# Attention on one Trainium2 core: mask sums, exponents and turned probabilities over 23 or 31 key columns instead of 24 or 32

## The chip, the cores and the metric

The kernel runs on one core of one Trainium2 chip. The time is device microseconds of one execution of the whole program. Before the change the median of three runs is 2007.32 us (2007.18 to 2007.69).

## The reference

The program computes a two-layer encoder on 1024 tokens of width 1024, in fp32. The tokens lie on a grid of 16 rows of 64 columns. In each layer eight heads of 64 features attend to a neighbourhood; other heads mix by a gated spatial matrix and by a Fourier transform; a projection and a SwiGLU feed-forward part follow. The part that matters here:

```python
kh, kw = 8, 16                     # each query sees 8 rows of 16 columns, clamped inside the grid
sc = einsum('bhjqd,bkjnhd->bhjqkn', q_row, k_band) * scale
logits = sc + bias                 # relative-position table; -1e9 outside the window
p = softmax(logits, axis=-1)
o = einsum('bhjqkn,bkjnhd->bjqhd', p, v_band)
```

## The kernel before, in words

Nearly all products are fp32 split into a high and a low part, three products for one. The attention of a layer lies between the last input product and the output projection. It is cut into eight tiles (`TILES`, line 56) of 128 queries: 8 grid rows by 16 grid columns. A tile is (j, rr): j is one of four column groups, rr the upper or the lower half of the rows. A tile's keys are 11 or 12 grid rows (`KR`) of `KC[j]` columns that start at column `BAND[j]`: 24, 32, 32 and 24 columns. So a head of a tile has 264, 288, 352 or 384 keys. They are worked in three chunks of four grid rows (`chunk`), 96 or 128 keys each, and the last one of an 11-row tile is shorter.

Work goes by pairs of heads, 32 pairs per layer (i in the code, four per tile). For each pair:

- TensorE makes the scores of both heads (`scores`, L2398, six products into two banks).
- VectorE adds the relative-position table and takes the negative maximum in one instruction per head (`logits`, L1772), reading the scores from PSUM and the table from SBUF and writing SBUF.
- ScalarE takes the exponent in place and its sum (`probs`, L1189).
- TensorE turns the probabilities chunk by chunk, 64 queries at a time (`turn_halves`, L2547; for the very first pair `turn_probs`, L2450).
- VectorE and ScalarE copy the turned halves to SBUF (L1809, L1214; first pair L1806, L1211).
- TensorE multiplies with the values (`values`, L2470): two heads, three chunks, six products, which the profile lists as twelve (two passes each).

After a tile VectorE, ScalarE and GpSimd norm its heads and TensorE turns them twice (L2485, L2492).

TensorE's order is written out by hand and it works in that order: `scores(i)`, `values(i - 2)`, sometimes a turn of other heads (`turn_batch`), `turn_halves(i - 1)`; from the fifth pair of pairs on (m in the code) two pairs at a time. An instruction that waits holds up all that is behind it on its engine.

The values come through DRAM: they are stored as `v_scratch` and loaded again with keys on partitions, by `load_rows(j)` (L678 to L682), one call for each column group. It has two buffers, `VB[j % 2]`. A call is four DMAs, one for each grid row modulo 4; each fills `KC[j]` partitions, from partition `r * KC[j]`, with four pieces of 512 floats (2048 bytes) per partition:

```python
sp.dma_start(VB[j % 2][r * KC[j]:(r + 1) * KC[j], :, :],
             vscr.rearrange("(n r w) d -> r w n d", r=CHUNK_ROWS, w=GW)[
                 r, BAND[j]:BAND[j] + KC[j]]).then_inc(vb_landed[j % 2], 16)
```

SyncE's queue issues in this order, and waits in it too: `load_rows(0)` when the values are stored; the tables of the third tile (its first half after four heads' mask sums of tile 0, its second half after eight); `load_rows(1)` once four batches are turned; the tables of the fourth tile; the first output weights; four 1 MB loads of the residual (`X`); `load_rows(2)` when the first two tiles' value products are done (`pv_done`), since it overwrites the first buffer; `load_rows(3)` when the next two tiles' are; the last tables. `values` waits for `vb_landed` before the first, third, fifth and seventh tile, that is for i = 0, 8, 16 and 24.

The relative-position tables (`bias`, laid out on the host by `lay_out`) have `KC[j]` columns per key row as well, are loaded by `load_bias` (L684 to L694) over 128 partitions, and are read by L1772.

Of the kernel before, what the change touches and what calls it, by code (L numbers as in the profile page):

```python
# [27 lines left out]
P = 128  # L28
# [3 lines left out]
DH = 64  # L32
# [12 lines left out]
KH, KW = 8, 16  # L45
QR, QC = 8, 16
KR = [11, 12]
KC = [24, 32, 32, 24]
CHUNK_ROWS = 4
NCHUNK = 3  # L50
NKEY = KR[1] * KC[1]
NJ = GW // QC
COMBO = [0, 1, 1, 2]
BAND = [min(max(QC * j - KW // 2, 0), GW - KC[j]) for j in range(NJ)]
NEG = -1e9
TILES = [(0, 1), (0, 0), (1, 0), (1, 1), (2, 1), (2, 0), (3, 0), (3, 1)]
BIAS_BUF = [0, 1, 0, 1, 1, 0, 1, 0]
# [129 lines left out]
def build(nc, x, win, wout, wom, wg, wu, wd, bias, wsp, bsp, lng, lnb, gmix, ghead, gffn, gfin,  # L187
          tw, bd, ident, out):
    ctx = ExitStack()
    with ctx:  # L190
        def at(name, kb, shape, dt=F32):
            return nc.alloc_sbuf_tensor_at(name, shape, dt, offset=BASE + int(kb * KB))
# [15 lines left out]
        MB, MC = UV[:, 0], XC[:, :, :]  # L208
        BIAS = [at(f"bias{n}", AT[f"BIAS{n}"], [P, 2, HA // 2 * NKEY]) for n in range(2)]
        SQB = [at(f"mix_sq{n}", AT[f"SQB{n}"], [P, 8, WB]) for n in range(2)]  # L210
# [14 lines left out]
        TW = at("twiddle", AT["TW"], [P, 5, 2, 256])  # L225
        L = at("logits", AT["L"], [P, 4, NKEY])
        OC = at("att_heads", AT["OT"], [P, NP, P])
# [26 lines left out]
        small = [200 * KB]  # L254
# [9 lines left out]
        shared = small[0]  # L264
# [8 lines left out]
        MV = keep("mean_var", [P, 8, 2])  # L273
        LR = keep("ln_rstd", [P, 8])
        PT = nc.alloc_sbuf_tensor_at("probs_t", [P, 4 * NCHUNK, P], F32, offset=BASE + shared)
        small[0] = shared + 4 * NKEY * 4
        for n, name in enumerate(("cu", "u4u", "t4")):
            HID[name] = nc.alloc_sbuf_tensor_at(f"hid_{name}", [P, HALF], F32, offset=BASE + shared + n * HALF * 4)
        GM = keep("g_mix", [P, KT_D])
# [14 lines left out]
        B = [ctx.enter_context(nc.psum_tensor(f"bank{i}", [P, HALF], F32)) for i in range(8)]  # L294

        def sem(name):
            return ctx.enter_context(nc.semaphore(name))
# [32 lines left out]
        s_full, l_made, p_made, pt_full, pt_dve, pt_act, pv_done = (  # L330
            sem(x) for x in ("s_full", "l_made", "p_made", "pt_full", "pt_dve", "pt_act", "pv_done"))
# [33 lines left out]
        def grid(ap):  # L365
            return ap.rearrange("p (r c) -> p r c", c=GW)
# [46 lines left out]
        def wait_tapped(e, l, n, j):  # L413

            if n == Z_GELU:
                e.wait_ge(z_ev, l * 8 + j + 1)
            elif n in ACT_TAPS:
                e.wait_ge(tap_act, l * 4 * len(ACT_TAPS) + 4 * ACT_TAPS.index(n) + j + 1)
            else:
                e.wait_ge(tap_dve, l * 4 * len(DVE_TAPS) + 4 * DVE_TAPS.index(n) + j + 1)  # L420
# [64 lines left out]
        def q_view(t, b):  # L485

            return t[:, b // 2, :].rearrange("p (j h r c) -> p h r j c", j=NJ, h=2, c=QC)[:, b % 2]

        def q_bank(b, ap):
            return ap.rearrange("p (r j c) -> p r j c", j=NJ, c=QC)  # L490

        BATCHES = [4, 5, 6, 7, 0, 1, 2, 3]
        BATCH_BANK = [4, 5, 7, 4, 5, 7, 4, 7]
        SINGLE = 8
# [14 lines left out]
        def keys(tile):  # L509
            j, rr = TILES[tile]  # L510
            return KR[rr] * KC[j]

        def chunk(tile, n):

            w = CHUNK_ROWS * KC[TILES[tile][0]]
            return slice(n * w, min((n + 1) * w, keys(tile)))

        def chunk_keys(tile, n):
            c = chunk(tile, n)
            return c.stop - c.start  # L520

        def score_bank(i, e):

            return B[e + 4 * (i >= SINGLE and i % 2)][:, 0:keys(i // 4)]

        def head_probs(t, n=None):

            first = t % 4 * NCHUNK
            return PT[:, first:first + NCHUNK, :] if n is None else PT[:, first + n, :]

        def half_probs(i, e):

            return PT[:, 2 * (i % 2) * NCHUNK:2 * (i % 2 + 1) * NCHUNK, e * DH:(e + 1) * DH]

        def turns_done(t):

            return t + 1 if t < 2 * WHOLE else t - t % 2 + 2
# [12 lines left out]
        def _(sp):  # L550
# [90 lines left out]
            for l in range(DEPTH):  # L641
# [36 lines left out]
                def load_rows(j):  # L678
                    for r in range(CHUNK_ROWS):
# [4 lines that stand above are left out]
# [225 lines left out]
        def _(act):  # L909
# [151 lines left out]
            for l in range(DEPTH):  # L1061
# [143 lines left out]
                def turned_odd(t):  # L1205
                    act.wait_ge(pt_full, l * 64 + t + 1)
                    if t >= 4:
                        act.wait_ge(pv_done, l * 64 + t - 3)
                    w = chunk_keys(t // 8, 0)
                    if t < 2 * WHOLE:  # L1210
                        nc.scalar.activation(head_probs(t)[0:w], B[3][0:w, 0:NKEY].rearrange("p (n q) -> p n q", q=P),  # L1211
                                             ACT.Copy).then_inc(pt_act, 1)
                    else:
                        nc.scalar.activation(half_probs(t // 2, 1)[0:w],  # L1214
                                             B[3][0:w, 0:NKEY].rearrange("p (g q) -> p g q", q=DH),
                                             ACT.Copy).then_inc(pt_act, 1)

                def batch_hi(i):
# [18 lines left out]
                for i in range(SINGLE):  # L1237
# [8 lines left out]
                    if 1 <= i < 5:  # L1246
                        c = i - 1
# [98 lines left out]
                for r in range(DN_STEPS):  # L1346
# [8 lines left out]
                    i = r - 58  # L1355
# [22 lines left out]
        def _(dve):  # L1378
# [136 lines left out]
            for l in range(DEPTH):  # L1515
# [126 lines left out]
                c = 0.5 ** 0.5  # L1642
# [119 lines left out]
                def logits(t):  # L1762

                    tile, h = divmod(t, 8)
                    dve.wait_ge(s_full, l * 64 + t + 1)
                    if t >= 4:
                        dve.wait_ge(pt_full, l * 64 + turns_done(t - 4))
                    if h % 4 == 0:
                        dve.wait_ge(bias_landed[BIAS_BUF[tile]][h // 4], l * 48 + 16 * BIAS_NTH[tile])
                    dve.sem_inc(dve_passed, 1)  # L1770

                    nc.vector.tensor_tensor_reduce(  # L1772
                        L[:, t % 4, 0:keys(tile)], score_bank(t // 2, t % 2),
                        BIAS[BIAS_BUF[tile]][:, h // 4, h % 4 * keys(tile):(h % 4 + 1) * keys(tile)], -1.0, 3e38,
                        ALU.add, ALU.min, NM[:, t % 4:t % 4 + 1]).then_inc(l_made, 1)

                logits(0)
                logits(1)
                tap(13, 2)
                head_norm(1, MB, SQB[0][:, :, :])  # L1780
# [19 lines left out]
                def turned_even(t):  # L1800
                    dve.wait_ge(pt_full, l * 64 + t + 1)
                    if t >= 4:
                        dve.wait_ge(pv_done, l * 64 + t - 2)
                    w = chunk_keys(t // 8, 0)
                    if t < 2 * WHOLE:
                        nc.vector.tensor_copy(head_probs(t)[0:w], B[2][0:w, 0:NKEY].rearrange("p (n q) -> p n q", q=P))\  # L1806
                            .then_inc(pt_dve, 1)
                    else:
                        nc.vector.tensor_copy(half_probs(t // 2, 0)[0:w],  # L1809
                                              B[2][0:w, 0:NKEY].rearrange("p (g q) -> p g q", q=DH)).then_inc(pt_dve, 1)  # L1810

                def batch_lo(i):
                    b = BATCHES[i]
# [367 lines left out]
                for r in range(DN_STEPS):  # L2181
# [3 lines left out]
                    i = r - 59  # L2185
# [37 lines left out]
        def _(pe):  # L2223
# [29 lines left out]
            for l in range(DEPTH):  # L2253
# [33 lines left out]
                for i, (k, h) in enumerate(X_ORDER):  # L2287
# [5 lines left out]
                    w = slice(k % 4 * WB, (k % 4 + 1) * WB)  # L2293
# [86 lines left out]
                def scores(i):  # L2380
                    tile, c = divmod(i, 4)
                    j, rr = TILES[tile]
                    if i > SINGLE + 1:
                        pe.wait_ge(l_made, l * 64 + 2 * i - 2)
                    elif i > SINGLE:
                        pe.wait_ge(bt_lo, l * 8 + 7)
                    elif i:
                        pe.wait_ge(l_made, l * 64 + 2 * i)
                    else:
                        pe.wait_ge(qk_lo, l * 16 + 12)  # L2390
                        wait_tapped(pe, l, NPROD - 1, 1)
                    if 4 <= i < 8:
                        pe.wait_ge(qk_lo, l * 16 + 8 + i + 1)
                    q0 = (2 * j + rr) * P
                    for n, (qs, ks) in enumerate(((QH, KH_), (QH, KL), (QL, KH_))):
                        for e in range(2):
                            hp = slice(DH * e, DH * e + DH)
                            mm = nc.tensor.matmul(  # L2398
                                score_bank(i, e).rearrange("p (r c) -> p r c", c=KC[j]), qs[hp, c, q0:q0 + P],
                                grid(ks[hp, c, :])[:, 4 * rr:4 * rr + KR[rr], BAND[j]:BAND[j] + KC[j]],  # L2400
                                start=n == 0, stop=n == 2)
                            if n == 2:
                                mm.then_inc(s_full, 1)
# [438 lines left out]
```

## Time and profile before

| | |
|---|---|
| median of the runs | 2007.32 us |
| the profiled execution | 2007.3 us |
| its span, first to last instruction | 2005.5 us |
| TensorE busy | 1981.8 us, 99% |
| VectorE busy | 1530.2 us, 76% |
| ScalarE busy | 895.3 us, 45% |
| GpSimd busy | 221.0 us, 11% |
| mean granted TensorE clock | 0.999 |

The profile is one execution on the chip. PE is TensorE's matmuls, PEld its weight loads, DVE VectorE, ACT ScalarE, POOL GpSimd, SPq SyncE's DMA queue. Times are in microseconds from the start of the span unless marked ns. An engine's busy time is a sum over stages with different limits, so the attention stages are read by themselves: the first is at about 198 to 276 us, the second at about 1189 to 1267 us. The share of DMA is the mean busy share of the core's 16 DMA engines; packets that overlap make it a little over 100% at times.

### The profile page before, as it was taken

The numbers are of one execution on the slowest core, as the hardware profiler recorded it, in microseconds if no ns is written. First come the engines' busy times: TensorE is split into PE (matmuls) and PEld (weight loads), VectorE is DVE, ScalarE is ACT, GpSimd is POOL, SyncE is SP. The second block draws the span as 40 slices with busy tenths as digits, with TensorE's granted clock in tenths as the row PEclk, the third lists the DMA queues.
The fourth block names the chain that finished last, engine by engine and source line by source line (L and its number), as shares of the span: only waits on it lengthen the run. The fifth ranks groups of instructions, "written<-read, shape, count | busy, mean of one in ns | idle before, by whom it ended". The sixth has DMA issues, their size and how long they took to land.

```text
span 2005.5 us, 28816 instructions
## 1 busy us (share of the span) xinstructions
PE 1981.8 (99%) x10528; PEld 1647.2 (82%) x10528; DVE 1530.2 (76%) x2511; ACT 895.3 (45%) x1611; POOL 221.0 (11%) x156
## 2 busy tenths in 40 slices
PE   8999999999999999999999999999999999999998
PEld 7887788888888888888898877888888888888887
DVE  8847874799777777787777488567997777778877
ACT  7453873443333333444544549535333333344443
POOL 1221453100000000000013123630000000000000
PEclk9999999999999999999999999999999999999999
DMA  7965743124432338533477668331343233293333
GB/s 247 214 168 154 228 156 119 43 99 170 132 110 90 106 109 288 174 98 96 120 220 193 156 159 245 138 105 58 129 157 118 90 106 110 100 342 99 95 100 122
DMA packets 130988, 288.91 MB, mean 144 GB/s; under 512 B 12960, under 2 KB 17952, under 8 KB 130592
## 3 DMA queue, kind: packets, MB, share of 16 engines
q1 hardware_dynamic: 107584, 241.97, 37.0%
q0 software_dynamic: 10880, 20.97, 6.3%
q10 hardware_dynamic: 12384, 24.12, 3.4%
q8 instruction: 85, 1.39, 0.3%
q14 instruction: 55, 0.45, 0.1%
HBM read 227.77 MB, written 59.24 MB: 143 GB/s over the span
## 4 chain that ended last, share of the span: by engine, by line
PE 89%; DVE 6%; issue 2%; ACT 2%; DMA 0%; DVEq 0%; SPq 0%; ACTq 0%
PE bank L2249 27%; PE bank L2251 27%; PE bank L2250 27%; PE bank L2470 1%; PE bank L2398 1%; PE bank L2547 1%; DVE s_lo L1484 1%; DVE t_lo L1913 0%; PE bank L2492 0%; PE bank L2361 0%; PE bank L2485 0%; ACT logits L1189 0%; PE bank L2377 0%; DVE logits L1772 0%; DVE att_sq L1829 0%
## 5 line engine op out<-in xcount | busy, mean ns | idle before, releaser
L2249 PE MATMUL bank<-t_hi,s_hi 128*128 128x512 f32 (+1 forms) x1336 | 516.9, 387 | 0.8 <-DVE hid_cu L2026 0.5
L2250 PE MATMUL bank<-t_lo,s_hi 128*128 128x512 f32 (+1 forms) x1336 | 516.3, 386 | 0.0
L2251 PE MATMUL bank<-t_hi,s_lo 128*128 128x512 f32 (+1 forms) x1336 | 516.3, 386 | 0.0
L2249 PEld LDWEIGHTS bank<-t_hi,s_hi 128*128 128x128 f32 x1336 | 250.9, 188 | 52.4 <-DVE hid_cu L2026 1.3
L2251 PEld LDWEIGHTS bank<-t_hi,s_lo 128*128 128x128 f32 x1336 | 250.9, 188 | 50.9
L2250 PEld LDWEIGHTS bank<-t_lo,s_hi 128*128 128x128 f32 x1336 | 251.0, 188 | 50.7
L2249 PE MATMUL bank<-b_hi,s_hi 128*128 128x512 f32 x528 | 206.0, 390 | 0.1
L2251 PE MATMUL bank<-b_hi,s_lo 128*128 128x512 f32 x528 | 205.5, 389 | 0.0
L2250 PE MATMUL bank<-b_lo,s_hi 128*128 128x512 f32 x528 | 205.4, 389 | 0.0
L992 ACT ACTIVATE s_hi<-w_u 128x512 fp32r<-128x512 f32 x142 | 89.6, 631 | 233.1 <-PE bank L2251 175.6
L992 ACT ACTIVATE s_hi<-w_down 128x512 fp32r<-128x512 f32 x154 | 97.3, 632 | 201.9 <-PE bank L2251 199.9
L1484 DVE TENSOR_TENSOR s_lo<-w_down,s_hi 128x512 fp32r<-128x512 f32 x154 | 107.7, 700 | 76.9 <-ACT s_hi L992 76.9
L992 ACT ACTIVATE s_hi<-w_g 128x512 fp32r<-128x512 f32 x142 | 89.4, 630 | 163.2 <-PE bank L2251 104.1
L827 POOL TENSOR_TENSOR w_lo<-w_raw,w_hi 128x1024 fp32r<-128x1024 f32 x34 | 85.7, 2532 | 691.8 <-ACT w_hi L932 580.1
L932 ACT ACTIVATE w_hi<-w_raw 128x1024 fp32r<-128x1024 f32 x91 | 92.8, 1053 | 68.3 <-DMA w_raw<-in_win 48.9
L2249 PEld LDWEIGHTS bank<-b_hi,s_hi 128*128 128x128 f32 x528 | 99.1, 188 | 21.3 <-issue 0.9
L2251 PEld LDWEIGHTS bank<-b_hi,s_lo 128*128 128x128 f32 x528 | 99.1, 188 | 20.7
L2250 PEld LDWEIGHTS bank<-b_lo,s_hi 128*128 128x128 f32 x528 | 99.2, 188 | 20.3
L1494 DVE TENSOR_TENSOR t_lo<-t_raw,t_hi 128x512 fp32r<-128x512 f32 x154 | 105.7, 687 | 6.3 <-ACT t_hi L998 6.1
L1484 DVE TENSOR_TENSOR s_lo<-w_g,s_hi 128x512 fp32r<-128x512 f32 x142 | 97.5, 686 | 10.6 <-ACT s_hi L992 10.6
L2249 PE MATMUL bank<-h_hi,w_hi 128*128 128x512 f32 x256 | 101.1, 395 | 0.0
L2251 PE MATMUL bank<-h_hi,w_lo 128*128 128x512 f32 x256 | 99.8, 390 | 0.0
(296 smaller groups left out, 3704.8 us busy)
## 6 DMA issues: line engine op xcount, KB each, us to landing
w_raw<-in_win SPq DMA_DIRECT2D x51, 512.0 KB, 5.8
w_g<-in_wg SPq DMA_DIRECT2D x44, 512.0 KB, 3.6
w_u<-in_wu SPq DMA_DIRECT2D x44, 512.0 KB, 4.5
t_raw<-hidden_t SPq DMA_DIRECT2D x88, 256.0 KB, 2.6
w_raw<-in_win POOLq DMA_DIRECT2D x40, 512.0 KB, 7.1
t_raw<-hidden_b SPq DMA_DIRECT2D x66, 256.0 KB, 2.6
hidden_b<-hid_g SPq DMA_DIRECT2D x60, 256.0 KB, 2.0
hidden_t<-hid_x SPq DMA_DIRECT2D x44, 256.0 KB, 2.0
```

The lines of the kernel that those rows point to most:

```text
L827: nc.gpsimd.tensor_tensor(WL[s][:, :], WR[s][:, :], WH[s][:, :], ALU.subtract).then_inc(w_ready, 1)
L932: nc.scalar.activation(WH[s][:, :], WR[s][:, :], ACT.Copy).then_inc(w_hi, 1)
L992: nc.scalar.activation(SH[q % W_RING][:, :], weight_block(q), ACT.Copy).then_inc(s_hi, 1)
L1484: nc.vector.tensor_tensor(SL[q % W_RING][:, :], weight_block(q), SH[q % W_RING][:, :], ALU.subtract)\
L1494: nc.vector.tensor_tensor(TL[t][:, :], TR[t][:, :], TH[t][:, :], ALU.subtract).then_inc(t_lo, 1)
L2249: nc.tensor.matmul(bank, lh, rh, start=start, stop=False, skip_group_check=reopened)
L2250: nc.tensor.matmul(bank, lh, rl, start=False, stop=False, skip_group_check=reopened)
L2251: return nc.tensor.matmul(bank, ll, rh, start=False, stop=stop, skip_group_check=reopened)
L2398: mm = nc.tensor.matmul(score_bank(i, e).rearrange("p (r c) -> p r c", c=KC[j]), qs[hp, c, q0:q0 + P], grid(ks[hp, c, :])[:, 4 * rr:4 * rr ...
L2470: mm = nc.tensor.matmul(B[VALUE_BANK][e * DH:(e + 1) * DH, c * P:(c + 1) * P], VB[j % 2][0:w, rr + n, h * DH:(h + 1) * DH], head_probs(h, ...
L2547: mm = nc.tensor.transpose(B[2 + e][0:chunk_keys(t // 8, n), (NCHUNK * s + n) * DH:(NCHUNK * s + n + 1) * DH], L[rows, t % 4, chunk(t // 8 ...
```

## The change

Column groups 0, 1 and 2 are cut to 23, 31 and 31 key columns (`KC`); their 24th or 32nd column is in no query's window. Group 3 keeps 24. The scores are still computed for 24, 32, 32 and 24 columns (`KS`) into the same places in PSUM. The mask sum reads from PSUM 23 or 31 of each 24 or 32 columns and writes rows of 23 or 31 without gaps. All that is sized by `KC`, and so needs no edit of its own, follows: the exponents, the chunks (92 or 124 keys), the turned probabilities, the value products, the tables in DRAM and their loads, and the partitions that `load_rows` fills. `NTURN` takes the place of `NKEY` where 384 turned elements are meant; the copies move what they moved, on 92 or 124 partitions.

```diff
-KC = [24, 32, 32, 24]
+KC = [23, 31, 31, 24]
+KS = [24, 32, 32, 24]
 CHUNK_ROWS = 4
 NCHUNK = 3
 NKEY = KR[1] * KC[1]
+NTURN = NCHUNK * P
@@
-        small[0] = shared + 4 * NKEY * 4
+        small[0] = shared + 4 * NTURN * 4
@@
         def score_bank(i, e):
-            return B[e + 4 * (i >= SINGLE and i % 2)][:, 0:keys(i // 4)]
+            j, rr = TILES[i // 4]
+            bank = B[e + 4 * (i >= SINGLE and i % 2)]
+            return bank[:, 0:KR[rr] * KS[j]].rearrange("p (r c) -> p r c", c=KS[j])
@@
-                        nc.scalar.activation(head_probs(t)[0:w], B[3][0:w, 0:NKEY].rearrange("p (n q) -> p n q", q=P),
+                        nc.scalar.activation(head_probs(t)[0:w], B[3][0:w, 0:NTURN].rearrange("p (n q) -> p n q", q=P),
@@
+                    def by_row(ap):
+                        return ap.rearrange("p (r c) -> p r c", c=KC[TILES[tile][0]])
+
                     nc.vector.tensor_tensor_reduce(
-                        L[:, t % 4, 0:keys(tile)], score_bank(t // 2, t % 2),
-                        BIAS[BIAS_BUF[tile]][:, h // 4, h % 4 * keys(tile):(h % 4 + 1) * keys(tile)], -1.0, 3e38,
+                        by_row(L[:, t % 4, 0:keys(tile)]), score_bank(t // 2, t % 2)[:, :, 0:KC[TILES[tile][0]]],
+                        by_row(BIAS[BIAS_BUF[tile]][:, h // 4, h % 4 * keys(tile):(h % 4 + 1) * keys(tile)]), -1.0, 3e38,
                         ALU.add, ALU.min, NM[:, t % 4:t % 4 + 1]).then_inc(l_made, 1)
@@
                             mm = nc.tensor.matmul(
-                                score_bank(i, e).rearrange("p (r c) -> p r c", c=KC[j]), qs[hp, c, q0:q0 + P],
-                                grid(ks[hp, c, :])[:, 4 * rr:4 * rr + KR[rr], BAND[j]:BAND[j] + KC[j]],
+                                score_bank(i, e), qs[hp, c, q0:q0 + P],
+                                grid(ks[hp, c, :])[:, 4 * rr:4 * rr + KR[rr], BAND[j]:BAND[j] + KS[j]],
                                 start=n == 0, stop=n == 2)
```

The other copies of turned probabilities get `NTURN` for `NKEY` in the same way. No instruction is added or removed, and no wait.

## Rows read from the trace of the kernel before

**Rows 1.** The page: busy time by engine, and the chain that ended last.
```profile
...
PE 1981.8 (99%) x10528; PEld 1647.2 (82%) x10528; DVE 1530.2 (76%) x2511; ACT 895.3 (45%) x1611; POOL 221.0 (11%) x156
...
PE 89%; DVE 6%; issue 2%; ACT 2%; DMA 0%; DVEq 0%; SPq 0%; ACTq 0%
...
```

**Rows 2.** Stretch of the first attention: busy us (instructions) per engine, clock, DMA, GB/s.
```profile
...
198.00:276.00 78.00, 74.38 (x1027) 59.86 (x1026) 67.43 (x193) 67.67 (x187) 27.32 (x25) 1.00 0.69 201
```

**Rows 3.** Groups by shape, same stretch: busy us, mean ns | idle before, releaser.
```profile
...
L1772 DVE CUSTOM_DVE_ANT_0 logits<-bank,bias 128x384 f32<-128x384 f32 x16 | 8.4, 551 | 0.4 <-PE bank L2398 0.4
L1772 DVE CUSTOM_DVE_ANT_0 logits<-bank,bias 128x264 f32<-128x264 f32 x16 | 6.3, 425 | 0.0
L1189 ACT ACTIVATE logits<-logits,minus_max 128x384 f32<-128x384 f32 x16 | 9.7, 608 | 0.7 <-DVE minus_max L1772 0.7
L1189 ACT ACTIVATE logits<-logits,minus_max 128x264 f32<-128x264 f32 x16 | 8.2, 511 | 1.1 <-DVE minus_max L1772 1.1
L2547 PE MATMUL bank<-ident,logits 64*128 64x64 f32 x160 | 8.9, 231 | 0.3 <-issue 0.2
L2547 PE MATMUL bank<-ident,logits 64*96 64x64 f32 x168 | 10.4, 222 | 0.0
L2470 PE MATMUL bank<-probs_t,v_band 128*64 128x128 f32 x160 | 11.6, 279 | 0.0
L2470 PE MATMUL bank<-probs_t,v_band 96*64 96x128 f32 x168 | 13.5, 279 | 1.6 <-ACT probs_t L1214 1.2 <-DVE probs_t L1809 0.2
...
```

**Rows 4.** Timeline of SyncE's queue, first layer: start, us from first to last issue.
```profile
...
198.35 1.57 SPq L680 DMA_DIRECT2D v_band<-v_scratch  x4
205.95 6.79 SPq L693 DMA_DIRECT2D bias<-in_bias  x2
212.78 2.10 SPq L680 DMA_DIRECT2D v_band<-v_scratch  x4
218.14 6.07 SPq L693 DMA_DIRECT2D bias<-in_bias  x2
...
224.72 2.28 SPq L710 DMA_DIRECT2D x_res<-in_x  x4
227.72 3.90 SPq L680 DMA_DIRECT2D v_band<-v_scratch  x4
```

**Rows 5.** Timeline of TensorE: first value products of tiles 0, 2 and 4.
```profile
...
208.00 0.88 PE L2470 MATMUL bank<-probs_t,v_band 96*64 96x128 f32 x12
...
229.84 1.07 PE L2470 MATMUL bank<-probs_t,v_band 128*64 128x128 f32 x14
...
247.19 1.08 PE L2470 MATMUL bank<-probs_t,v_band 128*64 128x128 f32 x14
```

**Rows 6.** DMA, 200.5 to 203.5 us: `load_rows(0)` moves, alone; queue: packets, MB, share.
```profile
...
DMA packets 275, 0.50 MB, mean 167 GB/s; under 512 B 30, under 2 KB 30, under 8 KB 275
...
q1 hardware_dynamic: 275, 0.50, 79.4%
...
```

**Rows 7.** DMA, 216.5 to 219.5 us: `load_rows(1)` moves.
```profile
...
DMA packets 355, 0.67 MB, mean 223 GB/s; under 512 B 38, under 2 KB 38, under 8 KB 353
...
q1 hardware_dynamic: 353, 0.65, 104.7%
...
```

**Rows 8.** DMA, 1192 to 1195.5 us: `load_rows(0)` of the second layer.
```profile
...
q1 hardware_dynamic: 342, 0.62, 74.9%
...
```

**Rows 9.** DMA, 770 to 780 us: feed-forward weights, pieces of 2048 bytes.
```profile
...
DMA packets 1985, 3.86 MB, mean 386 GB/s; under 512 B 99, under 2 KB 99, under 8 KB 1985
...
```

**Rows 10.** DMA, 229 to 236 us: the residual's loads.
```profile
...
q1 hardware_dynamic: 739, 2.88, 100.9%
...
```

**Rows 11.** Two stretches after the program's first matmul, columns as in rows 2.
```profile
...
7.00:10.00 3.00, 3.00 (x15) 3.00 (x16) 2.36 (x4) 3.00 (x6) 0.00 (x0) 1.00 1.03 367
11.00:14.00 3.00, 3.00 (x27) 3.00 (x27) 3.00 (x5) 3.00 (x5) 0.00 (x0) 1.00 1.05 387
...
```

More of the change, by code:

```diff
@@ L1214, in turned_odd @@
                         nc.scalar.activation(half_probs(t // 2, 1)[0:w],
-                                             B[3][0:w, 0:NKEY].rearrange("p (g q) -> p g q", q=DH),
+                                             B[3][0:w, 0:NTURN].rearrange("p (g q) -> p g q", q=DH),
                                              ACT.Copy).then_inc(pt_act, 1)
@@ L1805, in turned_even @@
                     if t < 2 * WHOLE:
-                        nc.vector.tensor_copy(head_probs(t)[0:w], B[2][0:w, 0:NKEY].rearrange("p (n q) -> p n q", q=P))\
+                        nc.vector.tensor_copy(head_probs(t)[0:w], B[2][0:w, 0:NTURN].rearrange("p (n q) -> p n q", q=P))\
                             .then_inc(pt_dve, 1)
@@ L1809, in turned_even @@
                         nc.vector.tensor_copy(half_probs(t // 2, 0)[0:w],
-                                              B[2][0:w, 0:NKEY].rearrange("p (g q) -> p g q", q=DH)).then_inc(pt_dve, 1)
+                                              B[2][0:w, 0:NTURN].rearrange("p (g q) -> p g q", q=DH)).then_inc(pt_dve, 1)
                 def batch_lo(i):
```

## The prediction

> **What bounds the kernel now.** I read the page first: TensorE is busy for 99% of the span and holds 89% of the chain that ended last [rows 1]. Then the stretch of the attention by itself, since the change is only there. In 78 us TensorE is busy 74.4, VectorE 67.4 and ScalarE 67.7 [rows 2]: three engines that hand heads to each other, none with much slack. The reader should see that a saving on one of them is worth at most itself. Next the groups by shape give the price of an element [rows 3]. Last, because the mask, the chunks and the value rows are sized by one constant, I read the loads that this constant also sizes: SyncE's queue in order of time [rows 4], the moments at which TensorE needs the value bands [rows 5], and the DMA engines while the bands move [rows 6 to 8].
>
> **The edits that were meant.** Mask sum: 384 keys take 551 ns and 264 take 425, so 1.05 ns a key [rows 3]. A 12-row tile loses 12 keys, an 11-row tile 11; 24 heads of each per layer give 24 x 12.6 + 24 x 11.6 = 0.58 us, 1.16 us in two layers. Exponent: (608 - 511) / 120 = 0.81 ns a key, 0.9 us in two layers [rows 3]. Turns: 128 columns take 231 ns, 96 take 222, so four columns are worth about 1.1 ns; 12 per pair of heads, 24 pairs, two layers: 0.6 us [rows 3]. Value products: 128 and 96 keys both take 279 ns, so nothing [rows 3]. The copies of turned probabilities move 384 elements as before, on fewer partitions: nothing, by the same reading. If all of this lay in series on the path it would be 2.7 us. It does not, the three engines overlap; I would take 1 us. The mask sum now reads PSUM in rows with a gap. No row of before shows that form at this line. Its bounds are nothing and one more element per row, 12 x 1.05 = 12.6 ns a head, which would just cancel its saving; I take nothing. The scores are as they were. The table loads keep 128 partitions and shrink by 3 or 4%: nothing.
>
> **The edit that comes along.** `load_rows` (L680) fills `KC[j]` partitions per DMA. That was 24 or 32 and becomes 23 or 31. How many DMA engines such a transfer uses can be read off. While the 24-partition loads move alone, the share is 79.4% in one layer and 74.9% in the other [rows 6, 8]; while the 32-partition loads move it is 104.7% [rows 7]. Their ratio is 0.72 to 0.76, and 12 of 16 engines is 0.75. The small packets agree. Packets under 512 B I take for the writes that report an engine's part as done, since no tile is moved in such pieces there. In [rows 6] there are 30 of them beside 245 others, one per 8.2 pieces. A 24-partition load has 24 x 4 = 96 pieces: on 12 engines 8 each, on 16 engines it would be 6. In [rows 7] it is 315 to 38, one per 8.3; 32 x 4 / 16 = 8. So each engine takes an equal share of whole partitions, and 12 and 16 are the largest counts up to 16 that divide 24 and 32. By that reading 23 and 31, which are primes, go to a single engine. The other reading that fits is two partitions per engine with an odd last share; nothing in these rows shows an uneven share. The Trainium skill (DMA: Bandwidth & Descriptors, section "Why a DMA increments its semaphore by 16 and not by 1") says that the hardware takes the largest count up to 16 that divides the slowest dimension of both sides, with 127 partitions on one engine as its example; the trace agrees for 24 and 32, and no row here shows a prime count. By that rule the sum below stands; by the other reading it would be that of rival (a).
>
> The price of a piece on one engine. The nearest clean row is the stretch of 2048-byte pieces at 770 us: 3.86 MB in 10 us on 16 engines, 0.0241 MB per engine and us, so 85 ns a piece [rows 9]. While the bands move it is worse: 0.794 x 3 us x 16 / 245 = 156 ns [rows 6]. There twelve engines write into 24 partitions at once; one engine by itself meets no such company, so I take 85 ns and keep 156 as the other end.
>
> The sum for the first layer, on the times of [rows 4, 5]:
> - `load_rows(0)`: 4 x 23 x 4 = 368 pieces x 85 ns = 31.3 us, from 198.35, with 1 us put on for start and landing (a guess): 230.7. The first value product stood at 208.00. TensorE waits, and scores, turns and all that VectorE and ScalarE live on are queued behind: a stall of 22.7 us.
> - `load_rows(1)` was issued at 212.78, 4.8 us after that product, because SyncE first waits for mask sums and turned batches that are behind it. So it comes at 235.5. Ahead of it on the same engine are 8 table rows of 5.5 KB, 44 KB, 2 us at the rate of [rows 10]. Then 4 x 31 x 4 = 496 pieces, 42.2 us, and 1 us: 280.6. Tile 2 needed it at 229.84 + 22.7 = 252.5: a stall of 28.1 us.
> - `load_rows(2)` was issued at 227.72 and comes at 250.4, while the engine is busy until 279.6. Ahead of it are that engine's parts of the tables of tile 3 (16 rows, 4 us), of the output weights (1.3) and of the residual: 4 MB / 16 at 2.88 MB per 7 us and 16 engines [rows 10] is 10.2 us. Then 42.2 and 1: 338 us. Tile 4 would follow tile 2 by 247.19 - 229.84 = 17.35 us, at 298.0: a stall of 40 us.
> - `load_rows(3)` keeps 24 partitions and its 12 engines, and follows at once. It is needed 17 us later: nothing.
>
> That is 91 us a layer, and 182 for both, since the second layer issues the same queue. The small savings of the first paragraph disappear under it: these stretches are bound by one DMA engine.
>
> A stall has a second cost. After its first 6.8 us without work TensorE ran 15 matmuls in 3 us, later 27 in 3 us of the same kind [rows 11], so it restarts at about half pace and loses some 1.7 us. The column of the granted clock says 1.00 in both, so the cause is not settled by it. The restart of tile 2 is covered by the load it waits for next; those of tiles 0 and 4 move the path: 3.4 us a layer, 7 us in all.
>
> Sum: the profiled execution has 2005.5 us of span and 1.8 us around it, 2007.3, which is also the median. 2007.3 + 182 + 7 = 2196.
>
> **The rivals.** (a) The loads spread as before, with an uneven last share. Then a band still moves in about 5 us, 0.75 MB at 0.50 MB in 3 us [rows 6], and what is left are the meant edits: 2007.3 - 1 = 2006.3, at best 2004.6. This is the case that is not slower; it decides by one thing, the share of DMA while `load_rows` moves. For it: 24 and 32 partitions had exactly two per engine. Against it: no uneven share in the trace. (b) One engine, but pieces at the 156 ns of [rows 6]. The bands take 57.4, 77.4 and 77.4 us: first band 256.8, a stall of 48.8; second 342, a stall of 63; third 435, a stall of 76; 188 a layer, 2390 in all with the restarts. For it: the only row in which these very bytes move. Against it: that row has many engines on few partitions. (c) The spread stays and the gapped rows cost VectorE more than I bound: for 0.2% it would have to be 4.0 us / 96 heads = 42 ns a head, beyond the bound. (d) The change is faster by over 0.2%: that needs 4.0 us, and all meant savings in series are 2.7.
>
> **How the numbers follow.** A change of 0.2%, 4 us, is about what can be told from none. Forecast with one engine near 85 ns: 0.68, 2196 us. (b), or a rate between: 0.14, up to 2390. (a): 0.11. (c) and other slower cases, such as few engines in place of one: 0.05. (d): 0.02. Slower is 0.68 + 0.14 + 0.05 = 0.87, same 0.11, faster 0.02. For the range, the lower bound of the forecast is the case in which the tables, weights and residual do not hold the third band up (15.5 us a layer) and restarts cost nothing: 2196 - 31 - 7 = 2158; a little less for a margin, 2145. The upper end is that of (b), 2390. It leaves out (a), (c), (d) and a sliver, under 2 in 10.
>
> **What the profile after would show.** While `load_rows(0)` moves the DMA share is near 1/16 = 6% for some 31 us, not 79% for 5; 3 stalls per layer before L2470, of about 23, 28 and 40 us, with `v_band` as what ended them; L1772 about 12 ns and L1189 about 10 ns shorter for 372 and 341 keys, for 276 and 253 too; L2470 unchanged at 279 ns; the fourth band as before. The prediction falls if the share during the bands stays above 70%, and its size falls if a piece takes other than 85 ns.

## The result and the profile after

The changed kernel takes 2206.95 us (median of four runs, 2206.15 to 2207.68) where the kernel before took 2007.39 us (median of four). The ratio is 1.099, with a 95% interval of 1.098 to 1.101. The profiled execution has a span of 2205.9 us. That is 199.6 us slower by the medians, 200.4 us by the spans.

The page after, with busy time, granted clock and the chain that ended last:

```profile
PE 1996.3 (90%) x10528; PEld 1661.4 (75%) x10528; DVE 1528.8 (69%) x2511; ACT 895.6 (41%) x1611; POOL 221.2 (10%) x156
...
PEclk9999668999999999999999986699999999999999
...
PE 78%; SPq 8%; DVE 6%; DMA 6%; issue 2%; ACT 1%; DVEq 0%; ACTq 0%
PE bank L2256 24%; PE bank L2258 24%; PE bank L2257 24%; SPq L684 6%; DMA v_band<-v_scratch 5%; SPq L697 1%; PE bank L2477 1%; SPq L714 1%; PE bank L2554 1%; DVE s_lo L1488 1%; PE bank L2405 1%; DMA v_scratch<-v_tok 0%; DVE t_lo L1920 0%; PE bank L2368 0%; PE bank L2499 0%
```

TensorE's share fell from 99% [rows 1] to 90%, and the clock row, all nines before, has two dips. SyncE's queue (SPq), its line L684 and the band of values are new in the chain. L684 is `load_rows`.

The list of waits names one new wait on TensorE. The columns are total us, times, longest:

```profile
PE bank L2477 <- DMA v_band<-v_scratch: 188.7, 6, 38.5
```

Six waits, three per layer, 188.7 of the 200.4 us. TensorE's timeline gives each by its place. These are the first value products of tiles 0, 2 and 4, which stood at 208.00, 229.84 and 247.19 before [rows 5]; the bracket is the idle time before them and its releaser:

```profile
231.24 1.55 PE L2477 MATMUL bank<-probs_t,v_band 92*64 92x128 f32 x12 [23.22 <-DMA v_band<-v_scratch]
...
286.52 1.76 PE L2477 MATMUL bank<-probs_t,v_band 124*64 124x128 f32 x14 [31.79 <-DMA v_band<-v_scratch]
...
344.35 2.40 PE L2477 MATMUL bank<-probs_t,v_band 124*64 124x128 f32 x20 [38.34 <-DMA v_band<-v_scratch]
```

SyncE's queue, which issued these loads at 198.35, 212.78 and 227.72 before [rows 4] (start, us from first to last issue):

```profile
198.08 15.80 SPq L684 DMA_DIRECT2D v_band<-v_scratch  x4
213.98 23.43 SPq L697 DMA_DIRECT2D bias<-in_bias  x2
237.45 24.96 SPq L684 DMA_DIRECT2D v_band<-v_scratch  x4
262.46 10.71 SPq L697 DMA_DIRECT2D bias<-in_bias  x2
...
273.86 8.74 SPq L714 DMA_DIRECT2D x_res<-in_x  x4
282.64 51.75 SPq L684 DMA_DIRECT2D v_band<-v_scratch  x8
```

And the DMA queue in the same three microseconds as rows 6:

```profile
DMA packets 35, 0.08 MB, mean 26 GB/s; under 512 B 0, under 2 KB 0, under 8 KB 34
...
q1 hardware_dynamic: 34, 0.07, 6.0%
```

Where 12 engines were busy (79.4%), about one is: 6.0% of 16 is 0.96 of an engine. There are 34 packets in 3 us, one every 88 ns.

The groups by shape answer to rows 3. The stretch holds stalls and half-clock work here, so TensorE's means are not those of an undisturbed stage:

```profile
L2477 PE MATMUL bank<-probs_t,v_band 124*64 124x128 f32 x160 | 13.7, 315 | 70.1 <-DMA v_band<-v_scratch 70.1
...
L1193 ACT ACTIVATE logits<-logits,minus_max 128x372 f32<-128x372 f32 x16 | 9.5, 599 | 1.3 <-DVE minus_max L1779 1.3
...
L2554 PE MATMUL bank<-ident,logits 64*124 64x64 f32 x160 | 9.4, 239 | 0.2
...
L1779 DVE CUSTOM_DVE_ANT_0 logits<-bank,bias 128x372 f32<-128x372 f32 x16 | 8.2, 539 | 0.7 <-PE bank L2405 0.7
```

The mask sum went from 551 to 539 ns and the exponent from 608 to 599. The meant edits did what they say, in a stage that now waits for something else.

### The profile page after: what moved, and what is told of

It is laid out like the page before. It is cut to its first block, busy times and chain, and to the rows that moved or that the text cites. A ratio compares the mean times of both kernels' runs of the same rounds, so it can differ in the third digit from the quotient of the medians.

```text
span 2205.9 us, 28816 instructions
## 1 busy us (share of the span) xinstructions
PE 1996.3 (90%) x10528; PEld 1661.4 (75%) x10528; DVE 1528.8 (69%) x2511; ACT 895.6 (41%) x1611; POOL 221.2 (10%) x156
## 4 chain that ended last, share of the span: by engine, by line
PE 78%; SPq 8%; DVE 6%; DMA 6%; issue 2%; ACT 1%; DVEq 0%; ACTq 0%
PE bank L2256 24%; PE bank L2258 24%; PE bank L2257 24%; SPq L684 6%; DMA v_band<-v_scratch 5%; SPq L697 1%; PE bank L2477 1%; SPq L714 1%; PE bank L2554 1%; DVE s_lo L1488 1%; PE bank L2405 1%; DMA v_scratch<-v_tok 0%; DVE t_lo L1920 0%; PE bank L2368 0%; PE bank L2499 0%
## 5 line engine op out<-in xcount | busy, mean ns | idle before, releaser
L2477 PE MATMUL bank<-probs_t,v_band 124*64 124x128 f32 (+5 forms) x768 | 58.9, 304 | 190.4 <-DMA v_band<-v_scratch 188.7
L2477 PEld LDWEIGHTS bank<-probs_t,v_band 124*64 124x64 f32 (+5 forms) x768 | 47.8, 152 | 197.9 <-issue 193.5
L1816 DVE COPY probs_t<-bank 124x384 f32<-124x384 f32 (+2 forms) x62 | 34.3, 553 | 211.0 <-PE bank L2554 210.4
L1218 ACT ACTIVATE probs_t<-bank 124x384 f32<-124x384 f32 (+2 forms) x62 | 29.7, 479 | 204.5 <-PE bank L2554 204.3
```

What stands on the lines that cost most here:

```text
L1218: nc.scalar.activation(half_probs(t // 2, 1)[0:w], B[3][0:w, 0:NTURN].rearrange("p (g q) -> p g q", q=DH), ACT.Copy).then_inc(pt_act, 1)
L1816: nc.vector.tensor_copy(half_probs(t // 2, 0)[0:w], B[2][0:w, 0:NTURN].rearrange("p (g q) -> p g q", q=DH)).then_inc(pt_dve, 1)
L2477: mm = nc.tensor.matmul(B[VALUE_BANK][e * DH:(e + 1) * DH, c * P:(c + 1) * P], VB[j % 2][0:w, rr + n, h * DH:(h + 1) * DH], head_probs(h, ...
```

## The experiments

**Part by part: only the first group, only the middle groups.** Both kernels differ from the changed one in one line.

```diff
-KC = [23, 31, 31, 24]
+KC = [23, 32, 32, 24]      # e3_only_23
+KC = [24, 31, 31, 24]      # e4_only_31
```

> The changed kernel with KC = 23, 32, 32, 24: only the first band is loaded over a prime number of partitions. Theory: the first stall of each layer stays (23 us) and the other two go; with 3 us for TensorE's slower restart that is 2007 + 2 x 26 = 2059 us. Rival, that the stalls come from something all narrowed tiles share: the time scales with the number of narrowed heads, 2 of 6 tiles, 2007 + 200 / 3 = 2074 us, and stalls stand before tiles 2 and 4 too.

> The changed kernel with KC = 24, 31, 31, 24: the first band loads as before. Theory: no first stall; the second band is issued at 212.8 us and lands near 212.8 + 3 + 42 = 258 us, needed at 230: a stall of 28 us; the third is queued behind it, the residual and the tables and lands near 317, needed at 275: 41 us. 2007 + 2 x (28 + 41 + 3) = 2151 us. Rival of shared cause: 4 of 6 tiles, 2007 + 133 = 2140 us, with stalls inside the tiles and not only before the value products of tiles 2 and 4.

Measured: 2060.1 us and 2156.4 us. The waits for the bands, first of e3_only_23 and then of e4_only_31:

```profile
PE bank L2477 <- DMA v_band<-v_scratch: 46.8, 2, 23.6
```

```profile
PE bank L2477 <- DMA v_band<-v_scratch: 142.8, 4, 39.4
```

Two waits of 23 us with 23 columns, four of 32 to 39 us with 31, and none where the load is over 24 or 32 partitions. The two parts add up: 52.8 + 149.1 = 201.9 us against 199.6 together. The expectations were 2059 and 2151 us. The rivals of a shared cause (2074 and 2140 us) fall, on the time by 14 and 16 us and on the place of the waits.

**The load alone, computation untouched.**

```diff
+PART = {24: 23, 32: 31}
-                        sp.dma_start(VB[j % 2][r * KC[j]:(r + 1) * KC[j], :, :], ...)
+                        for a, b in ((0, PART[KC[j]]), (PART[KC[j]], KC[j])):
+                            sp.dma_start(VB[j % 2][r * KC[j] + a:r * KC[j] + b, :, :], ...)
```

(In TensorE's wait for the band, eight loads are counted instead of four.)

> The kernel before, masks, chunks and sums untouched, with each band load of 32 partitions cut into 31 and 1, and each of 24 into 23 and 1. Theory: 31, 23 and 1 all go to one engine, which then moves 384, 512 and 512 pieces for 368, 496 and 496; 16 pieces more are 1.4 us per band, 8 us in all, and the meant savings of 1 us are absent: 2207 + 9 = 2216 us. Rival, the narrowed computation is part of the cost: clearly below 2207 us.

Measured: 2243.2 us. With masks, chunks and sums as before, the loss is there in full: nothing that was narrowed is needed for it. The waits for bands over the whole run:

```profile
PE bank L2472 <- DMA v_band<-v_scratch: 180.8, 6, 35.5
```

The size I missed, by 27 us. The sum of the expectation left out what the fourth band costs, which the edit cuts too, 24 partitions into 23 and 1, and which the changed kernel does not. What that does in the first layer stands in the stretch from 350 to 390 us, in which there is a wait that is not for a band at all:

```profile
DVE logits L1774 <- DMA bias<-in_bias: 19.3, 1, 19.3
PEld bank L2472 <- DVE probs_t L1811: 18.8, 1, 18.8
```

SyncE's queue shows why. The columns are start and us from first to last issue:

```profile
283.12 79.68 SPq L682 DMA_DIRECT2D v_band<-v_scratch  x16
362.85 2.80 SPq L695 DMA_DIRECT2D bias<-in_bias  x4
```

The 16 issues of the third and fourth band stretch over 80 us (part of it is the wait for value products between the two), and the tables of the last tiles, issued at 362.85, come too late for VectorE's mask sum. Over both layers VectorE waits 39.2 us for these tables, in two waits. A load on one engine costs whoever is behind it in the queue that issues it, and not only who waits for its data.

**The load mended, computation as changed.** Each load is cut in two by the loop of e2_before_31_1, so that by the largest divisor each part goes to 11 to 16 engines:

```diff
+PART = {23: 12, 31: 16, 24: 12}    # e1_split, on the changed kernel: 12+11, 16+15, 12+12
+PART = {24: 12, 32: 16}            # e5_before_16_16, on the kernel before: 12+12, 16+16
```

> The changed kernel with each band load of 31 partitions cut into loads of 16 and 15, of 23 into 12 and 11, of 24 into 12 and 12 (eight loads a band instead of four). Theory, one engine for a prime number of partitions: every load then spreads over 11 to 16 engines, a band moves in about 5 to 8 us, the six stalls before the value products go, and the time falls from 2207 us to that of the kernel before less the meant savings, 2005 to 2008 us. Rival, the mask sums over rows with gaps or the odd chunk sizes hold the path: the time stays above 2050 us, and mask sums of 372 keys or turns are slower than the 539 and 239 ns they took in the changed kernel.

> The kernel before with its band loads cut in two (32 into 16 and 16, 24 into 12 and 12), nothing else. It is the control of e1_split: whatever eight loads in place of four cost is in both. Expected within 0.1% of before (2006 to 2009 us), since each engine moves the same pieces. e1_split against this one is the meant edits alone: theory 1 us faster (2.7 at most), rival nothing or slower.

Measured: 2008.24 us for e1_split (2006.66 to 2011.73, ratio 1.0005, interval 0.9996 to 1.0014) and 2008.63 us for its control (ratio 1.0012, 1.0003 to 1.0021). The first is 0.2 us above the 2005 to 2008 us that I expected. The six stalls are gone, and of 189 us of waits for bands one is left in e1_split:

```profile
PE bank L2479 <- DMA v_band<-v_scratch: 1.0, 1, 1.0
```

Both kernels scatter over 5 and 9 us where the kernel before scatters over 1.2 us, so they don't resolve an edit worth 1 us. The control is 1.3 us slower than before, and its interval leaves 1 out, so there the cut is not free.

**A looser third band.** The same pair with the residual's four loads issued behind the third band's load, and the changed kernel itself with that order alone:

```diff
-                for k in range(0, KT_D, 2): sp.dma_start(X[:, k:k + 2, :], ...)
-                for j in (2, 3):
-                    sp.wait_ge(pv_done, l * 64 + 16 * (j - 1))
-                    load_rows(j)
+                sp.wait_ge(pv_done, l * 64 + 16)
+                load_rows(2)
+                for k in range(0, KT_D, 2): sp.dma_start(X[:, k:k + 2, :], ...)
+                sp.wait_ge(pv_done, l * 64 + 32)
+                load_rows(3)
```

> The changed kernel with cut band loads (as e1_split) and the four loads of the residual issued behind the third band's load instead of ahead of it, so that the third band no longer lands only half a us before its use. Theory: the meant edits then show, at most 2.7 us and about 1: 2005.5 us. Rival: the path through the attention is TensorE's own work, which the edits leave alone, and the time is that of its control e9_before_split_x_behind within 0.3 us.

> The kernel before with the same cut loads (16 and 16, 12 and 12) and the residual's loads behind the third band's: the control of e8_split_x_behind. Theory: what the cut cost in e5_before_16_16 (1.3 us) was the third band landing too late, so this one is back at 2006.5 to 2007.3 us with a narrow spread. Rival: the cost is the eight issues themselves, and it stays at 2008.5.

> The changed kernel, band loads as they are in it, with the four loads of the residual issued behind the third band's load. Theory, the residual's share of engine 0 (10 us) stands ahead of the third band, and slows the tail of the second by some 2 us: both go, 12 us a layer, 2183 us. Rival, only the pieces of the bands themselves count: 2207 us.

Measured: e8_split_x_behind 2007.00 us (2006.53 to 2008.41; ratio 0.9998, 0.9989 to 1.0007), its control 2009.41 us (2006.81 to 2013.07; ratio 1.0010, 1.0002 to 1.0019). The control did not come back to 2007 and still scatters, so the theory that the cut's cost was the third band's lateness falls; its rival, the eight issues, gave 2008.5. I had expected e8_split_x_behind at 2005.5 us, 1.5 us less than it took. What makes the control scatter is open. The pair differs by 2.4 us in favour of the narrowed kernel, but with a control that moves by 6 us I don't take that for the worth of the edits. Neither beats the kernel before by more than the measurement tells.

e7_x_behind took 2189.5 us, 17.4 less than the changed kernel, where I expected 24. First value products of tiles 2 and 4:

```profile
283.43 0.91 PE L2478 MATMUL bank<-probs_t,v_band 124*64 124x128 f32 x6 [26.00 <-DMA v_band<-v_scratch]
...
334.22 2.19 PE L2478 MATMUL bank<-probs_t,v_band 124*64 124x128 f32 x18 [31.14 <-DMA v_band<-v_scratch]
```

The third stall fell from 38.3 to 31.1 us. The second band landed 3.1 us earlier (283.43 for 286.52) and the third 10.1 us earlier (334.22 for 344.35), where 12 was expected. So the residual's share of that one engine was part of the cost, as the sum had it. The rival, that only the bands' pieces count, falls.

The second stall fell by 5.8 us, more than the 3.1 us of its band, and the rest is not the edit. After the first stall TensorE's granted clock stays 0.50 until about 245 us in this profile, and until 237 in that of the changed kernel, though nothing ahead of it differs. So TensorE comes to the second wait 2.7 us later. e2_before_31_1 and e3_only_23, with the same first stall, also show 0.50 until about 245. How long the low clock lasts behind the same stall varies between executions, and here the next wait hides it.

**Which rule gives the number of engines.**

```diff
+                        for a, b in {24: ((0, 24),), 32: ((0, 25), (25, 32))}[KC[j]]:
```

> The kernel before with each band load of 32 partitions cut into 25 and 7; those of 24 stay whole. Three readings of how many engines a load gets. Largest count up to 16 that divides the partitions: 5 and 7 engines; the fullest engine moves 20 + 4 = 24 pieces per grid row, 96 a band, 8 us at 85 ns. The second band still lands in time, the third lands 2 to 6 us late: 2010 to 2020 us. One engine whenever the count is not a multiple of 8: 128 pieces per grid row on engine 0 and stalls like those of the changed kernel in the second and third band, about 2150 us. Uneven shares on all engines: within 2 us of before.

Measured: 2028.1 us (2027.08 to 2029.62; ratio 1.011, 1.009 to 1.012). While the second band moves:

```profile
DMA packets 220, 0.44 MB, mean 147 GB/s; under 512 B 18, under 2 KB 18, under 8 KB 218
...
q1 hardware_dynamic: 218, 0.42, 42.0%
```

42.0% of 16 engines are 6.7: between the one engine of a non-multiple of 8 and the 16 of uneven shares, and near the 7 of the largest divisor, if the 5 engines of one part are among the 7 of the other. The small packets say the same. 128 pieces of a grid row, as 25 and 7 partitions on 5 and 7 engines, would end in 12 of them, one per 10.7; on one engine for each part in 2, one per 64; with two partitions per engine and an odd last share in 13 and 4, one per 7.5. The row has 18 beside 202, one per 11.2. The waits for bands:

```profile
PE bank L2471 <- DMA v_band<-v_scratch: 17.2, 2, 9.2
```

This picks the largest divisor among the three readings. The size is above the 2010 to 2020 us I gave: the third band ended 9.2 and 8.0 us late. I had priced its pieces at 85 ns, and the row above says otherwise: 202 data packets in 0.42 x 3 us x 16 are 100 ns each, before the load meets the residual's and the tables'.

**The meant edits alone.** The bands are loaded as before, in shape and in place:

```diff
-                        sp.dma_start(VB[j % 2][r * KC[j]:(r + 1) * KC[j], :, :], ... r, BAND[j]:BAND[j] + KC[j]
+                        sp.dma_start(VB[j % 2][r * KS[j]:(r + 1) * KS[j], :, :], ... r, BAND[j]:BAND[j] + KS[j]
```

> The changed kernel with band loads of 24 and 32 partitions, four a band and exactly as before, each grid row at its old partition. Left out: the value products then multiply some keys with the wrong value rows, so the attention's output is not the reference's; no instruction, shape or wait differs from the changed kernel but the loads. It is the meant edits alone, without the wide spread that cut loads brought. Theory: about 1 us faster than before, 2006.3 us, at most 2.7 us. Rival, odd starts, rows with gaps or chunks of 92 and 124 cost something: 2007.5 us or more.

Measured: 2007.09 us (2006.76 to 2008.96) against 2007.35 us, ratio 0.9999, interval 0.9991 to 1.0008. By shape in its first attention:

```profile
L2477 PE MATMUL bank<-probs_t,v_band 124*64 124x128 f32 x160 | 11.6, 279 | 0.0
L1193 ACT ACTIVATE logits<-logits,minus_max 128x372 f32<-128x372 f32 x16 | 9.6, 600 | 0.8 <-DVE minus_max L1779 0.7
...
L2554 PE MATMUL bank<-ident,logits 64*124 64x64 f32 x160 | 8.8, 228 | 0.2
L1779 DVE CUSTOM_DVE_ANT_0 logits<-bank,bias 128x372 f32<-128x372 f32 x16 | 8.2, 539 | 0.4 <-PE bank L2405 0.4
```

Against rows 3 the mask sum is 12 ns shorter, the exponent 8, the turn 3, the value product the same. The total lies between the 2006.3 us of the theory and the 2007.5 of the rival, and its interval includes no change at all. The last value products of the second attention start here, first e11_wide_bands, then the kernel before:

```profile
1269.42 1.53 PE L2477 MATMUL bank<-probs_t,v_band 96*64 96x128 f32 x24
```

```profile
1269.82 1.53 PE L2470 MATMUL bank<-probs_t,v_band 96*64 96x128 f32 x24
```

That is 0.40 us earlier, with two layers' narrowed heads behind it. But it is one profiled execution of each, and the runs of the kernel before alone differ by 0.9 us. It hints at less than the 1 us that I took, and doesn't show a gain. This kernel was made for its time only; a right one that loads the wide bands was not built.

**TensorE's clock.** The changed kernel with small matmuls in front of the three waits, and each wait moved behind TensorE's other waits of that place:

```diff
+                        for _ in range({0: 150, 8: 210, 16: 255, 24: 0}[i]):     # e10_busy
+                        for _ in range({0: 100, 8: 132, 16: 172, 24: 0}[i]):     # e12_busy_less
+                            nc.tensor.matmul(B[VALUE_BANK][:, 0:P], IDENT[:, :], IDENT[:, :], start=True, stop=True)
                         pe.wait_ge(vb_landed[j % 2], ...)
```

> The changed kernel with 150, 210 and 255 small fp32 matmuls (identity by identity, into the bank that the value products overwrite next) in TensorE's queue ahead of the waits for the first, second and third band, so that TensorE is not idle while it waits. Theory, part of the 11 us that the stalls do not explain is TensorE at half clock after each: the granted clock stays 1.00 and the time falls by 4 to 10 us, to 2197 to 2203 us. Rival, the extra is something else (queues filling up again): no change, or longer by what the added matmuls overrun.

> As e10_busy, with 100, 132 and 172 of the small matmuls ahead of the waits for the first, second and third band: at 0.225 us each, as e10_busy showed, 22.5, 29.7 and 38.7 us, just inside the stalls of the changed kernel. Theory: the granted clock stays at 1.00, the work after the first and third band runs at the pace of before, and the time falls from 2207 us by 2 x (2.5 + 2.5) = 10 us, to 2197 us. Rival, the extra beyond the stalls is not TensorE's clock: within 2 us of 2207, or above it.

e10_busy took 2281.2 us. I had counted 0.15 us for one of them. The timeline shows 300 passes, two for each of 150, in 33.7 us, so 0.225 us each, and they overran the stalls:

```profile
208.16 33.74 PE L2473 MATMUL bank<-ident 128*128 128x128 f32 x300
```

With the counts mended e12_busy_less took 2197.7 us (2196.78 to 2198.19), 9.3 us less than the changed kernel, near the 10 us of its theory. In its profile TensorE still waits up to 2.8 us for a band behind the added matmuls, so they did not overrun. Right behind the first and third band the changed kernel works like this. The columns are length, busy us (instructions) of PE, PEld, DVE, ACT and POOL, granted clock, DMA share, GB/s:

```profile
231.30:237.00 5.70, 5.70 (x48) 4.43 (x50) 2.33 (x6) 2.29 (x5) 0.64 (x1) 0.50 0.01 4
238.00:244.00 6.00, 5.41 (x76) 4.06 (x74) 5.32 (x14) 5.61 (x16) 2.73 (x3) 1.00 0.42 133
344.40:349.90 5.50, 5.50 (x48) 4.84 (x50) 0.56 (x1) 0.78 (x2) 0.00 (x0) 0.50 0.06 23
350.00:356.00 6.00, 6.00 (x100) 5.18 (x98) 5.33 (x16) 4.53 (x14) 2.00 (x3) 1.00 0.31 98
```

and e12_busy_less, in the same two places:

```profile
231.30:237.00 5.70, 5.07 (x72) 3.93 (x71) 4.54 (x12) 4.50 (x12) 1.32 (x2) 1.00 0.18 39
344.00:350.00 6.00, 6.00 (x98) 5.23 (x94) 3.86 (x12) 4.12 (x13) 0.18 (x1) 1.00 0.13 29
```

Granted clock 0.50, the 1.2 GHz level, and 48 matmuls in 5.7 and 5.5 us after a stall; at 1.00, the 2.4 GHz level, 72 and 98 in 5.7 and 6 us in the same places where TensorE had been kept busy. So most of the 10.9 us that the stalls did not explain (199.6 less 188.7) is TensorE's clock.

## Why the prediction was right, point by point

- **The load that comes along, the number of engines.** Right. The share of DMA was 6.0%, the loss is there with the load alone (e2_before_31_1), it is gone when the load is mended (e1_split) or wide (e11_wide_bands), and 25 and 7 partitions come between (e6_before_25_7). The prediction had this from the ratio of the shares and from one completion packet per eight pieces. Rival (a), uneven shares, falls. The Trainium skill (DMA: Bandwidth & Descriptors, section "Why a DMA increments its semaphore by 16 and not by 1") gives the largest common divisor up to 16 as the rule; the trace agrees for 23 by the share of 6.0%, for 31 by the 6.5% shown under the next point, and for 25 with 7 by the share of 42.0%.
- **The price of a piece.** Taken at 85 ns, measured at 88 by the packets of the first band. Rival (b), 156 ns, does not hold while one engine moves alone. But it has a core: the tail of the second band is that slow. Two stretches of the changed kernel, 262 to 272 us, where the second band moves alone, and 276 to 284 us, beside the residual's loads:

```profile
DMA packets 125, 0.25 MB, mean 25 GB/s; under 512 B 1, under 2 KB 1, under 8 KB 125
...
q1 hardware_dynamic: 125, 0.25, 6.5%
...
DMA packets 781, 3.06 MB, mean 382 GB/s; under 512 B 51, under 2 KB 51, under 8 KB 781
```

  In the first, 124 data packets in 10 us are 81 ns each on one engine, with one small packet beside them: 31 x 4 = 124 is a whole load of 31 partitions, reported once. In the second all engines together move 382 GB/s, most of it the residual. From 241.5 to 273 us the same view has 394 data packets of this queue, of the 496 pieces of the band, and by estimate ten came before; so some 90 are left for the last 13.5 us, about 150 ns each (an estimate from these counts). "One engine by itself meets no such company" was therefore wrong for this tail. e7_x_behind shows the residual's part in it: without its loads the band lands 3.1 us earlier. Why a piece takes longer in company is open.
- **The three stalls.** First layer, forecast 22.7, 28.1 and 40 us; measured 23.2, 31.8 and 38.3. The second is the term that was mis-sized, by 3.7 us, and the cause is its transfer: 49.1 us from the issue at 237.45 to the landing, where 45.1 was forecast, because its tail met other loads. Without the residual (e7_x_behind) it is 46.0 us. Its issue was also 2 us later than the 235.5 of the forecast, since the work ahead of it ran at half clock (with TensorE kept busy, in e12_busy_less, it was issued at 235.24). But for the same reason tile 2 needed it 2.2 us later, so that counts as a restart and not in the stall. The third was counted 2 us too long: TensorE took 19.5 us from tile 2 to tile 4 and not 17.35, which is the restart of tile 2 that the wait covers, as forecast. Sum per layer 93.3 where 91 was forecast, and 95.3 in the second layer, which I had set equal to the first; its second stall was 33.3 us, and no run says why. So 188.7 instead of 182 us.
- **The restarts.** Forecast 7 us, from a start at half pace in rows 11 whose cause was left open. e12_busy_less gives 9.3 us and the cause for the restarts here: the granted clock, at 0.50 for some 6 us after the first stall and after the third, where rows 11 had 3 us of half pace. In rows 11 the clock column reads 1.00, so nothing shows that it is the same effect. The 1.7 us came from a row that may be of another kind, and that it lies near the measured 2.3 us a restart is in part luck.
- **The meant edits.** For 372 keys the mask sum and the exponent are 12 and 8 to 9 ns shorter, as priced; the turn is 3 ns shorter where 1.1 was priced; the value product is unchanged. The gapped rows cost nothing that shows: the mask sum of 276 and 253 keys is also 9 to 16 ns shorter, in this kernel, e1_split and e11_wide_bands. Taken at 1 us on the path if nothing were in front; e11_wide_bands can't tell them from no change, so this term is neither confirmed nor refuted.
- **The sum.** 2196 forecast, 2206.95 measured: 6.7 us from the stalls, 2.3 from the clock, and about 2 us that no run assigns.

## What to carry to other kernels

When a size shrinks, look for every transfer that has it as its outermost dimension, and count divisors before elements: here a band with 4% less to load, 23 partitions for 24, took 33 us from its issue where it had taken about 6, because 23 can't be split evenly. Before costing compute edits that are worth a us, read the DMA share while each affected load moves. If a narrowed load can't be avoided, cut it into parts whose counts divide well: 12 with 11 and 16 with 15 brought 2207 back to 2008 us, though with more scatter than before. Loading the old width and computing on the new took as little time in e11_wide_bands, but its value products read wrong rows, so a right kernel of that form is untested. None of them was faster than the kernel before.

## What was not expected of the hardware

- Issues to one engine hold up the queue that issues them. SyncE took 15.8 us from the first to the end of the fourth issue of the first band, where it took 1.57 us before [rows 4], and 25.0 us for the second, where it took 2.10. That moved loads behind it that have nothing to do with the bands (e2_before_31_1: tables 19.3 us late for VectorE).
- Right behind waits of 23 and 38 us TensorE's granted clock is 0.50 in the rows, and 9.3 us of 2207 came back when it was kept busy with matmuls that nobody needs. Behind the same 23 us the low clock lasted until 237 us in one execution and until about 245 in three others.
- Cutting the kernel before's loads into 16 and 16 and 12 and 12 made its runs scatter over 9 and 6 us (e5_before_16_16, e9_before_split_x_behind). The same cut in the changed kernel scattered over 5 us (e1_split), and over 1.9 us with the residual moved (e8_split_x_behind). Why is open.
